# A two-block model of mixers and 16384 experts on one core: how the experts' choice, its weights and the first convolution tap are shared out among the engines

## The chip, the core and the metric

The kernel runs on one core of one Trainium2 chip. The time is the device time of one execution in microseconds, and the median of three runs is compared. The engines are TensorE (PE in the rows), VectorE (DVE), ScalarE (ACT), GpSimd (POOL) and SyncE (SP), which issues most of the transfers.

## What is computed

Two layers of a first block and two of a second, on 256 tokens of width 1024, all in float32. The change touches the first block alone, whose two layers each do:

```python
h = rms_norm(x, norm1_g[l]) * (1.0 + sc1) + sh1
z, xbc, dt_raw, mq, mk, mv, sq, sk, sv = jnp.split(h @ w_in[l], offsets, axis=-1)
# ssd_mixer begins with: xbc = silu(causal_depthwise_conv(xbc, conv_w, conv_b)), 4 taps, 1024 channels
y = concatenate([ssd_mixer(...), moba_attention(...), swa_attention(...)], -1) @ w_out[l]
x = x + g1 * y
h = rms_norm(x, norm2_g[l]) * (1.0 + sc2) + sh2
x = x + g2 * peer_ffn(h, peer_wq[l], peer_k1[l], peer_k2[l], peer_u[l], peer_v[l])
```

and `peer_ffn`, for each token, with 8 heads and 16 of 128 x 128 experts:

```python
q = (xc @ wq).reshape(PEER_CHUNK, PEER_HEADS, 2, PEER_HALF)
s1 = einsum("thd,nd->thn", q[:, :, 0], k1);  s2 = einsum("thd,nd->thn", q[:, :, 1], k2)
v1, i1 = lax.top_k(s1, 16);  v2, i2 = lax.top_k(s2, 16)
cand = (v1[..., :, None] + v2[..., None, :]).reshape(..., 256)
sc, ci = lax.top_k(cand, 16)
e = take(i1, ci // 16) * 128 + take(i2, ci % 16)
g = softmax(sc)
pre = einsum("td,thkd->thk", xc, u[e])
act = gelu(pre) * g
return einsum("thk,thkd->td", act, v[e])
```

## The kernel before

**Parts.** Every weight matrix comes as parts of 128 x 2048 values (1 MB) that SyncE loads into four raw buffers, in one order for the whole kernel. So that TensorE can multiply float32 values in its fast format, each part is split: ScalarE copies it into a rounded upper half (`upper_part`, L1487), and raw minus upper makes the lower half (`lower_part`, L1980 on VectorE, or L766 on GpSimd). There are two buffers for upper halves and two for lower ones, so a lower half of part n can be written only when TensorE is done with part n - 2. TensorE multiplies upper by both halves of the activations and lower by the upper half: `by_feature` (L838, L844) with 32 + 16 matmuls of 256 columns, or `doubled_by_feature` (L886 to L896) with 16 of 512 columns, that take both halves of the activations at once and put them side by side into a bank, and 16 of 256. The second form uses two PSUM banks a part, whose halves must be added afterwards.

**Experts.** All experts are computed densely. 64 parts hold `u` and 64 hold `v`; `expert_order` gives 40 parts of `u` (2 x AHEAD) and then alternates pairs of the two. The gates, a 128 x 128 array for each token that is zero but for the chosen experts, are made as a product of two one-hot matrices (`hot(i)` on VectorE, L2370 and L2371, for eight tokens; `gate_group(i)` on TensorE, L1188; `gates(i)` on ScalarE, L1675), 32 groups a layer. SyncE spills them and fetches them back (`spill`, `fetch`).

**The choice.** While TensorE works on the first LEAD = 21 parts of `u`, VectorE chooses: `best_16` takes maxima, indices and replaced values by groups (L2300 to L2310), first in the 32 groups of scores, then in 16 groups of candidate sums (L2319); then the gate subtraction (L2326), index arithmetic (L2332 to L2343), and two passes of compare, multiply and reduce over 4096 elements (L2347, L2350, L2353) that look up the keys, and the softmax sum, which signals `chosen` (L2359). During this time VectorE makes no lower halves: GpSimd makes those of parts 0 to 22. Then TensorE transposes the chosen numbers (L1178), VectorE copies them (L1960), makes hot(0) and hot(1), and from then on a step is one part and two groups, for 16 steps, and VectorE makes the lower halves again, two parts ahead.

**Ahead of the choice.** The eight query parts (`wq`) are multiplied by `parts_by_feature`, and the results are taken from PSUM by VectorE and ScalarE in turn. When all eight are out, TensorE multiplies by the keys (L1146), eight banks of four groups, and the two engines take these in turn as well. All eight must be out before the first maximum.

**The convolution.** ScalarE takes the four parts of `xbc` into `xpad` (L1578). VectorE then makes four taps in turn (L2109 for the first with the bias, L2112 for the others), with lower halves and the step sizes of the state space part between them; their result is needed for the segment sums (L2156 to L2158 on VectorE, L1046 to L1048 on TensorE).

Order on each engine is that of the program; engines meet only at semaphores. `free`, `filled` and `emptied` are those of a PSUM bank, `p_.upper()`, `p_.lower()`, `p_.lower_free()` and `p_.done()` those of a part.

## Time and profile before

| | us |
|---|---|
| median of three runs | 3445.7 |
| lowest and highest run | 3445.4 and 3454.18 |
| span of the profiled execution | 3444.9 |
| TensorE busy | 3323.0 |
| VectorE busy | 2474.5 |
| ScalarE busy | 1557.9 |
| GpSimd busy | 241.5 |

The busy times are of one profiled execution on the one core, whose mean granted TensorE clock is 0.984 of full speed. A row of a timeline gives the start, the duration, the engine, the line of the kernel, the operation with its output and inputs, how often it stands there, and in brackets the engine's idle time before it and what ended it. Matmuls overlap, so the mean duration of one is longer than the distance to the next.

### The profile page before, as it was taken

The numbers are of one execution on the slowest core, as the hardware profiler recorded it, in microseconds if no ns is written. First come the engines' busy times: TensorE is split into PE (matmuls) and PEld (weight loads), VectorE is DVE, ScalarE is ACT, GpSimd is POOL, SyncE is SP. The second block draws the span as 40 slices with busy tenths as digits, with TensorE's granted clock in tenths as the row PEclk, the third lists the DMA queues.
The fourth block names the chain that finished last, engine by engine and source line by source line (L and its number), as shares of the span: only waits on it lengthen the run. The fifth ranks groups of instructions, "written<-read, shape, count | busy, mean of one in ns | idle before, by whom it ended". The sixth has DMA issues, their size and how long they took to land. (4 is left out here: it accounts for less than half of the span.)

```text
span 3444.9 us, 50906 instructions
## 1 busy us (share of the span) xinstructions
PE 3323.0 (96%) x20214; PEld 2943.0 (85%) x20214; DVE 2474.5 (72%) x4259; ACT 1557.9 (45%) x1835; POOL 241.5 (7%) x56
## 2 busy tenths in 40 slices
PE   7999999999999999999999999999999999999998
PEld 4889999888888899998888878888878788888787
DVE  7879996777887669986667777566657575655575
ACT  3544454343334444454443345453455454544543
POOL 0018400000000039000000000000000000000000
PEclk9999999999999999999999999999999999999999
DMA  9454467778874244566667765543445455434453
GB/s 377 169 181 172 175 224 270 276 275 280 288 272 160 102 167 167 193 238 228 214 213 240 243 251 188 195 147 123 159 150 194 166 205 198 150 133 147 149 188 142
DMA packets 172164, 689.64 MB, mean 200 GB/s; under 512 B 12396, under 2 KB 78724, under 8 KB 99223
## 3 DMA queue, kind: packets, MB, share of 16 engines
q1 hardware_dynamic: 167492, 663.86, 54.4%
q10 hardware_dynamic: 4436, 22.53, 1.8%
q8 instruction: 161, 2.64, 0.3%
q14 instruction: 75, 0.61, 0.0%
HBM read 650.66 MB, written 35.68 MB: 199 GB/s over the span
## 5 line engine op out<-in xcount | busy, mean ns | idle before, releaser
L1487 ACT ACTIVATE weights_upper<-weights 128x2048 fp32r<-128x2048 f32 x520 | 996.1, 1916 | 1546.3 <-issue 467.6
L1980 DVE TENSOR_TENSOR weights_lower<-weights,weights_upper 128x2048 fp32r<-128x2048 f32 x474 | 1084.4, 2289 | 553.2 <-ACT weights_upper L1487 553.0
L838 PE MATMUL ps<-hT_span,weights_upper 128*128 128x256 f32 x4992 | 636.4, 285 | 1.5 <-ACT hT_span L1777 1.2
L838 PEld LDWEIGHTS ps<-hT_span,weights_upper 128*128 128x128 f32 x4992 | 615.1, 193 | 9.0 <-issue 3.5
L890 PE MATMUL ps<-hT_span,weights_upper 128*128 128x512 f32 x1440 | 343.5, 391 | 0.0
L844 PE MATMUL ps<-hT_span,weights_lower 128*128 128x256 f32 x2496 | 325.4, 283 | 4.2 <-POOL weights_lower L766 4.2
L766 POOL TENSOR_TENSOR weights_lower<-weights,weights_upper 128x2048 fp32r<-128x2048 f32 x46 | 238.5, 5200 | 1141.3 <-ACT weights_upper L1487 1141.3
L844 PEld LDWEIGHTS ps<-hT_span,weights_lower 128*128 128x128 f32 x2496 | 310.7, 192 | 5.2 <-POOL weights_lower L766 5.2
L890 PEld LDWEIGHTS ps<-hT_span,weights_upper 128*128 128x128 f32 x1440 | 264.6, 188 | 51.2
L1228 PE MATMUL ps<-weights_upper,hidden_lower 128*128 128x512 f32 x1008 | 250.7, 391 | 0.0
L1228 PE MATMUL ps<-weights_upper,hidden_upper 128*128 128x512 f32 x1008 | 249.0, 389 | 0.0
L1228 PE MATMUL ps<-weights_lower,hidden_upper 128*128 128x512 f32 x1008 | 248.9, 389 | 0.0
L1228 PEld LDWEIGHTS ps<-weights_upper,hidden_lower 128*128 128x128 f32 x1008 | 187.1, 188 | 45.4 <-ACT weights_upper L1487 7.8
L1228 PEld LDWEIGHTS ps<-weights_upper,hidden_upper 128*128 128x128 f32 x1008 | 189.2, 188 | 39.3
L1228 PEld LDWEIGHTS ps<-weights_lower,hidden_upper 128*128 128x128 f32 x1008 | 189.2, 188 | 39.3
L896 PEld LDWEIGHTS ps<-hT_span,weights_lower 128*128 128x128 f32 x1536 | 196.5, 191 | 7.0
L896 PE MATMUL ps<-hT_span,weights_lower 128*128 128x256 f32 x1536 | 199.3, 283 | 0.0
L2371 DVE TENSOR_SCALAR scr<-cst,scr 128x128 f32<-128x128 f32 x512 | 172.2, 336 | 0.0
L2370 DVE TENSOR_SCALAR scr<-cst,scr 128x128 f32<-128x128 f32 x512 | 149.6, 292 | 0.2
L1188 PE MATMUL ps<-scr 128*128 128x128 f32 x1024 | 130.7, 284 | 7.1 <-DVE scr L2371 7.1
L1188 PEld LDWEIGHTS ps<-scr 128*128 128x128 f32 x1024 | 124.4, 198 | 11.1 <-DVE scr L2371 7.8
L2390 DVE TENSOR_TENSOR hidden_upper<-work,scr 128x512 fp32r<-128x512 f32 x80 | 55.4, 692 | 92.8 <-PE ps L1228 92.7
(400 smaller groups left out, 3967.4 us busy)
## 6 DMA issues: line engine op xcount, KB each, us to landing
weights<-in_parts SPq DMA_DIRECT2D x264, 1024.0 KB, 4.8
weights<-in_experts SPq DMA_DIRECT2D x256, 1024.0 KB, 4.9
scr<-gates SPq DMA_DIRECT2D x32, 1024.0 KB, 8.4
work<-in_ada_s SPq DMA_DIRECT2D x96, 256.0 KB, 5.3
gates<-h SPq DMA_DIRECT2D x16, 1024.0 KB, 4.8
gates<-work SPq DMA_DIRECT2D x16, 1024.0 KB, 4.8
weights<-in_ada_w SPq DMA_DIRECT2D x6, 2048.0 KB, 15.3
scr<-in_ada_l SPq DMA_DIRECT2D x35, 256.0 KB, 5.6
```

The lines of the kernel that those rows point to most:

```text
L766: g.tensor_tensor(lower[:, p_.r % SPLIT, :], raw[:, p_.r, :], upper[:, p_.r % SPLIT, :].bitcast(F32), ALU.subtract).then_inc(lower_ready, 1)
L838: m = mm(bank[:, e * T:(e + 1) * T], up[:, c, e * P:(e + 1) * P], s_[:, c, :], start=(e == 0 and n == 0 and c == 0), stop=False, skip_grou ...
L844: m = mm(bank[:, e * T:(e + 1) * T], lo[:, c, e * P:(e + 1) * P], src[0][:, c, :], start=False, stop=(c == KC - 1), skip_group_check=True)
L890: m = mm(banks[e].rearrange("p (n t) -> p n t", n=2), w[:, c, :], both[c], start=(c == 0), stop=False, skip_group_check=True)
L896: m = mm(banks[e][:, T:2 * T], lo[:, c, e * P:(e + 1) * P], src[0][:, c, :], start=False, stop=(c == KC - 1), skip_group_check=True)
L1188: m = mm(k.bank("G", j)[:, t * P:(t + 1) * P], hotA[:, i % 2, 4 * j + t, :], hotB[:, i % 2, 4 * j + t, :], start=True, stop=True, skip_gro ...
L1228: m = mm(k.bank("acc", 2 * t_ + dh), src[:, u, c, t_ * P:(t_ + 1) * P], w[:, c, dh * NBLK:(dh + 1) * NBLK], start=False, stop=False, skip_ ...
L1487: f(upper[:, p_.r % SPLIT, :], raw[:, p_.r, :], ACT.Copy).then_inc(upper_ready, 1)
L1980: v.tensor_tensor(lower[:, s, :], raw[:, p_.r, :], upper[:, s, :].bitcast(F32), ALU.subtract)\
L2370: v.tensor_scalar(hotA[:, i % 2, j, :], iota, ET[:, 0, t:t + 1], None, ALU.is_equal)
L2371: m = v.tensor_scalar(hotB[:, i % 2, j, :], iota, ET[:, 1, t:t + 1], ET[:, 2, t:t + 1], ALU.is_equal, ALU.mult)
L2390: v.tensor_tensor(tokens(hid_up[:, u, :, :]), act_, g_, ALU.mult)
```

## The change

- LEAD is 20 instead of 21, and of the parts before the steady step GpSimd makes only the lower halves 0 to 10 (POOLED = 11). VectorE makes part 11 behind the bit operations, 12 and 13 behind compare and multiply of the first pass, 14 and 15 behind its reduction, 16, 17 and 18 likewise in the second pass, 19 and 20 behind `chosen`, and 21 behind hot(0).
- The gate groups are shifted: group 0 with part LEAD, groups 1 and 2 with the next, and so on (`groups_behind`), and `hot` signals after four tokens instead of eight.
- The query parts use `doubled_by_feature`: 16 fills of a bank instead of 8, ScalarE copies the first half, VectorE adds the second.
- The score banks are filled in the order of the query pieces, each when its four pieces are ready; ScalarE takes all of them, and VectorE takes the first eight maxima of a bank as soon as it is out.
- ScalarE makes the convolution's first tap, two channels' groups behind each take, and the parameters' semaphore is split for it.

```diff
-LEAD = 2 * CHOOSE + 1
+LEAD = 2 * CHOOSE
+POOLED = 11
...
-    p.fill("wq", 8, parts=1)
+    p.fill("wq", 16, last=[i // 2 for i in range(16)])
...
+def groups_behind(n):
+    return range(max(2 * (n - LEAD) - 1, 0), max(min(2 * (n - LEAD) + 1, GROUPS), 0))
...
-                    if 0 <= n - LEAD - RAW < GROUPS // 2:
-                        spill(n - LEAD - RAW)
+                    if 0 <= n - LEAD - RAW - 1 < GROUPS // 2:
+                        spill(n - LEAD - RAW - 1)
                     if n == LEAD + RAW + GROUPS // 2 + 1:
                         fetch(0)
                         fetch(1)
...
                 g.wait_ge(*part(firsts[l], 0, "wq", 7).lower())
-                for n in range(LEAD + SPLIT):
+                for n in range(POOLED):
...
                 for i in range(8):
-                    parts_by_feature(k, 0, "wq", i, src=hT1, fresh=(k, "h2T", "upper1", l * 12 + 8))
+                    doubled_by_feature(k, 0, "wq", i, (k, "h2T", "upper1", l * 12 + 8), src=hT1, both=hT1_both)
                 for i in range(8):
-                    pe.wait_ge(*k.emptied("wq", i))
-                for i in range(8):
-                    t, hp = i // 4, i % 4
+                    hp, t = i // 2, i % 2
+                    for c in range(4 * hp, 4 * hp + 4 if t == 0 else 4 * hp):
+                        pe.wait_ge(*k.emptied("wq", c))
...
-                    pe.wait_ge(S("hot"), l * GROUPS + (i + 1))
                     for j in range(2):
+                        pe.wait_ge(S("hot"), l * (2 * GROUPS) + (2 * i + j + 1))
...
                 for n in range(LEAD, 2 * AHEAD):
                     first_layer(n, *order[n][1:])
-                    if n < LEAD + GROUPS // 2:
-                        for i in range(2):
-                            gate_group(2 * (n - LEAD) + i)
+                    for i in groups_behind(n):
+                        gate_group(i)
...
                     take(k, "xbc", i, xpad[:, 2 * i:2 * i + 2, 3:259])
+                    if i == 0:
+                        act.wait_ge(S("col1_in"), l * 16 + 16)
+                    act.drain()
+                    for c in (2 * i, 2 * i + 1):
+                        m = f(conv[:, c, :], xpad[:, c, 0:T], ACT.Identity, scale=colp[:, K1["cw"] + 4 * c:][:, 0:1],
+                              bias=colp[:, K1["cb"] + c:][:, 0:1])
+                    m.then_inc(S("first_tap"), 1)
...
-                for i in range(1, 8, 2):
-                    ahead("wq", i - 1, 2)
-                    take(k, "wq", i, qT[:, 2 * i:2 * i + 2, :])
+                for i in range(8):
+                    ahead("wq", i)
+                    for e in range(2):
+                        act.wait_ge(*k.filled("wq", 2 * i + e))
+                        act.sem_inc(S("held"), 1)
+                        m = f(qT[:, 2 * i + e, :], k.bank("wq", 2 * i + e)[:, 0:T], ACT.Copy)
+                    m.then_inc(S("wq_first"), 1)
...
-                for i in range(1, 8, 2):
-                    take(k, "s", i, sc[:, 4 * i:4 * i + 4, :])
+                for i in range(8):
+                    g_ = 16 * (i % 2) + 4 * (i // 2)
+                    take(k, "s", i, sc[:, g_:g_ + 4, :])
...
-                for i in range(4):
-                    v.wait_ge(*k.emptied("xbc", i))
-                for tap in range(4):
-                    if tap:
+                for tap in range(1, 4):
+                    if tap > 1:
                         v.drain()
                     for c in range(8):
                         w = colp[:, K1["cw"] + 4 * c + tap:][:, 0:1]
-                        if tap == 0:
-                            m = v.tensor_scalar(conv[:, c, :], xpad[:, c, 0:T], w,
-                                                colp[:, K1["cb"] + c:K1["cb"] + c + 1], ALU.mult, ALU.add)
...
+                        if tap == 1 and c % 2 == 0:
+                            v.wait_ge(S("first_tap"), l * 4 + (c // 2 + 1))
+                        m = v.scalar_tensor_tensor(out=conv[:, c, :], in0=xpad[:, c, tap:tap + T], scalar=w,
+                                                   in1=conv[:, c, :], op0=ALU.mult, op1=ALU.add)
-                    if tap == 0:
+                    if tap == 1:
                         ahead("wint", 0)
-                    elif tap == 1:
                         ahead("wint", 1)
...
-                for i in range(0, 8, 2):
-                    ahead("wq", i, 2)
-                    take(k, "wq", i, qT[:, 2 * i:2 * i + 2, :])
-                    late_pieces(36 + 2 * i, 4 if i < 6 else 0)
-                for i in range(0, 8, 2):
-                    take(k, "s", i, sc[:, 4 * i:4 * i + 4, :])
-
                 for i in range(8):
-                    v.wait_ge(*k.emptied("s", i))
-                v.sem_inc(S("held"), 1)
+                    ahead("wq", i)
+                    late_pieces(36 + 2 * i, 2 if i < 6 else 0)
+                    v.wait_ge(S("wq_first"), l * 8 + (i + 1))
+                    v.sem_inc(S("held"), 1)
+                    for e in range(2):
+                        v.tensor_tensor(qT[:, 2 * i + e, :], k.bank("wq", 2 * i + e)[:, T:2 * T], qT[:, 2 * i + e, :],
+                                        ALU.add).then_inc(k.empty_sem("wq", 2 * i + e), 1)
...
+                for i in range(8):
+                    v.wait_ge(*k.emptied("s", i))
+                    v.sem_inc(S("held"), 1)
+                    g_ = 16 * (i % 2) + 4 * (i // 2)
+                    largest_8(range(g_, g_ + 4), sc, V16)
                 best_16(32, sc, sc2, V16, I16u)
...
+                v.wait_ge(*expert_part(l, 0, POOLED - 1).lower())
+                lower_part(expert_part(l, 0, POOLED))
...
                 for e in range(2):
+                    n = POOLED + 1 + 4 * e
                     v.drain()
                     v.tensor_tensor(onehot[:, :, :], column(Cf[:, e, :], PK), row(iota[:, 0:PK], 256), ALU.is_equal)
+                    lower_part(expert_part(l, 0, n))
...
+                    lower_part(expert_part(l, 0, n + 1))
                     v.drain()
                     v.tensor_reduce(E3[:, e, :], onehot[:, :, :], AX.X, ALU.add)
+                    for i in range(n + 2, n + 4 - e):
+                        lower_part(expert_part(l, 0, i))
...
                 v.tensor_tensor(gate, gate, column(stat(248, 16), PK), ALU.mult).then_inc(S("chosen"), 1)
+                for n in range(POOLED + 8, LEAD + 1):
+                    lower_part(expert_part(l, 0, n))
...
-                    m.then_inc(S("hot"), 1)
+                        if j % 4 == 3:
+                            m.then_inc(S("hot"), 1)
...
                 hot(0)
-                hot(1)
-                v.wait_ge(*expert_part(l, 0, LEAD + SPLIT - 1).lower())
+                lower_part(expert_part(l, 0, LEAD + 1))
...
-                    i = 2 * (n - LEAD) + 2
-                    if i < GROUPS:
+                    for i in groups_behind(n + 1) if n < EXPERTS - 1 else ():
                         hot(i)
-                        hot(i + 1)
```

## Rows read from the trace of the kernel before

**Rows 1.** Page, busy us of an engine (share) xcount; costliest groups: busy, mean ns | idle.

```profile
PE 3323.0 (96%) x20214; PEld 2943.0 (85%) x20214; DVE 2474.5 (72%) x4259; ACT 1557.9 (45%) x1835; POOL 241.5 (7%) x56
...
L1980 DVE TENSOR_TENSOR weights_lower<-weights,weights_upper 128x2048 fp32r<-128x2048 f32 x474 | 1084.4, 2289 | 553.2 <-ACT weights_upper L1487 553.0
```

**Rows 2.** TensorE's waits in the whole span: us in total, times, longest.

```profile
PE ps L1188 <- DVE scr L2371: 7.1, 3, 3.1
...
PE ps L1046 <- DVE scr L2158: 5.9, 2, 4.0
...
PE ps L844 <- POOL weights_lower L766: 4.2, 4, 1.5
...
PE ps L1146 <- ACT work L1470: 1.8, 2, 0.9
```

**Rows 3.** Timeline of TensorE, layer 0: start us, us, engine, line, operation.

```profile
256.40 4.00 PE L838 MATMUL ps<-hT_span,weights_upper 128*128 128x256 f32 x32
...
262.16 4.00 PE L838 MATMUL ps<-hT_span,weights_upper 128*128 128x256 f32 x32
...
374.18 0.82 PE L1178 MATMUL ps<-cst,scr 128*128 128x128 f32 x6
374.76 4.07 PE L838 MATMUL ps<-hT_span,weights_upper 128*128 128x256 f32 x32
...
390.23 4.08 PE L838 MATMUL ps<-hT_span,weights_upper 128*128 128x256 f32 x32
```

**Rows 4.** Windows, one steady step: length, busy us (x) of each engine, clock, DMA.

```profile
390.23:399.74 9.51, 9.51 (x83) 9.40 (x82) 9.51 (x35) 4.81 (x7) 0.00 (x0) 1.00 0.63 221
```

**Rows 5.** Timeline of TensorE, layer 1.

```profile
1260.68 4.00 PE L838 MATMUL ps<-hT_span,weights_upper 128*128 128x256 f32 x32
...
1378.79 0.82 PE L1178 MATMUL ps<-cst,scr 128*128 128x128 f32 x6
...
1395.51 4.49 PE L838 MATMUL ps<-hT_span,weights_upper 128*128 128x256 f32 x32
```

**Rows 6.** Timeline of GpSimd: part 10 of layer 0, last eight parts of layer 1.

```profile
302.80 4.62 POOL L766 TENSOR_TENSOR weights_lower<-weights,weights_upper 128x2048 fp32r<-128x2048 f32 x1 [1.13 <-ACT weights_upper L1487]
...
1335.89 49.01 POOL L766 TENSOR_TENSOR weights_lower<-weights,weights_upper 128x2048 fp32r<-128x2048 f32 x8 [1.01 <-ACT weights_upper L1487]
```

**Rows 7.** Timeline of VectorE, layer 0, second half of the choice.

```profile
309.37 4.10 DVE L2326 TENSOR_TENSOR scr<-scr 128x256 f32<-128x256 f32 x1
...
326.60 8.70 DVE L2347 TENSOR_TENSOR position_hot<-scr,cst 128x4096 bf16<-128x4096 f32 x1
...
342.00 4.42 DVE L2353 TENSOR_REDUCE scr<-position_hot 128x256 f32<-128x4096 bf16 x1
...
375.94 4.43 DVE L2370 TENSOR_SCALAR scr<-cst,scr 128x128 f32<-128x128 f32 x1
```

**Rows 8.** Timeline of VectorE, layer 1: compare and multiply of the first pass.

```profile
1335.50 4.42 DVE L2347 TENSOR_TENSOR position_hot<-scr,cst 128x4096 bf16<-128x4096 f32 x1
1340.00 6.57 DVE L2350 TENSOR_TENSOR position_hot<-position_hot,chosen_keys 128x4096 bf16<-128x4096 bf16 x1
```

**Rows 9.** Timeline of TensorE, second block: two upper passes of the doubled form.

```profile
2061.18 3.82 PE L890 MATMUL ps<-hT_span,weights_upper 128*128 128x512 f32 x16
...
2066.75 3.82 PE L890 MATMUL ps<-hT_span,weights_upper 128*128 128x512 f32 x16
```

**Rows 10.** Groups of instructions by line: busy us, mean ns | idle before.

```profile
L1470 ACT ACT_TABLE_LOAD x8 | 10.3, 1283 | 0.1
...
L1660 ACT ACTIVATE work<-ps 128x256 f32<-128x256 f32 x24 | 7.8, 376 | 0.0
```

**Rows 11.** Timeline of ScalarE, layer 1, behind the xbc parts.

```profile
1096.44 1.92 ACT L1487 ACTIVATE weights_upper<-weights 128x2048 fp32r<-128x2048 f32 x1 [2.34 <-PE ps L941]
```

**Rows 12.** Timeline of VectorE, layer 1: the first tap and the second weight part.

```profile
1091.58 2.67 DVE L2109 TENSOR_SCALAR work<-work,colp 128x256 f32<-128x256 f32 x8
...
1099.72 2.29 DVE L1980 TENSOR_TENSOR weights_lower<-weights,weights_upper 128x2048 fp32r<-128x2048 f32 x1
```

24 lines of the change are left out of this document (12 added, 12 removed).

## The prediction, made before the changed kernel ran

> **What bounds the kernel.** I read the page's table of busy time first: TensorE is busy for 96% of the span [rows 1], so the time is the matrix work plus the places where TensorE waits. The view of waits then names them, and the ones this change can touch are four [rows 2]: L1188 (gate groups) on VectorE's one-hots, 7.1 us; L844 (lower parts) on GpSimd, 4.2 us; L1146 (key scores) on ScalarE, 1.8 us; L1046 (segment sums) on VectorE, 5.9 us, 4.0 of it in layer 1, so 1.9 in layer 0. Waits understate a stall, since steps between them stretch too; so I took TensorE's timeline around the choice and compared it with its own rhythm. A first-layer part takes 5.76 us from start to start [rows 3]. Part 1 begins at 256.40, so part 21 would come 20 x 5.76 = 115.2 us later, at 371.6; the transposes L1178 that precede it start at 374.18: 2.6 us lost. From there to part 22 at 390.23 are 16.05 us. The same work undisturbed is 0.58 (transposes, 374.18 to 374.76) and one full step with two gate groups, 9.51 [rows 4]: 10.09. So 6.0 more are lost, 8.6 in layer 0. Layer 1 [rows 5]: 1378.79 against 1260.68 + 115.2 = 1375.9 is 2.9; 16.72 against 10.09 is 6.6; 9.5 together. In the steady step VectorE is busy for all its 9.51 us, so TensorE and VectorE are level there [rows 4], and nothing is to be had in it.
>
> **Why it is lost.** GpSimd's subtraction takes 4.62 us when alone, on TensorE's beat of 5.76. But the last eight, in layer 1 from 1335.89, take 49.01 us, 6.1 each [rows 6]. VectorE's side shows the partner [rows 7]: the gate subtraction at 309.37 ends at 313.47, just behind GpSimd's part 11 (302.80 + 5.76 + 4.62 = 313.18); the compare of 4096 elements takes 8.70 at 326.60, and 4.42 in layer 1 where GpSimd asks only afterwards [rows 6, 8]; the multiply takes 6.57 [rows 8]; the first one-hot at 375.94 takes 4.43, where the 32 of a steady step have (9.51 - 2.29) / 32 = 0.23 each [rows 1, 4], and it holds up hot(0) and so the gate groups. Each long row is its own work plus the rest of a GpSimd instruction. The Trainium skill (SBUF, State Buffer, "two separate sides") has this as a rule: the port pair that VectorE and GpSimd share is locked for a whole instruction, and an operation with two SBUF inputs takes part in it. The rows agree.
>
> **The change, part by part**
>
> 1. **Lower parts 11 to 21 on VectorE.** GpSimd keeps 0 to 10. Part 10 at 302.80 ends at 307.42 [rows 6], before the gate subtraction. From there no VectorE operation meets GpSimd. I cost the late choice in that state: from the gate subtraction to the compare 17.23 us now, of which the gate's own wait is 313.18 - 309.37 = 3.8 and two more GpSimd instructions of 4.62 are waited for (parts 12 and 13, the cast L2334 and L2339), so 4.2 remain; then for each of two passes compare 4.42, multiply, reduce 4.42 [rows 7, 8]. The multiply is bounded by 6.57 above; in layer 1 the compare ends at 1339.92, GpSimd then works 4.62 to 1344.5, and the multiply that began at 1340.00 ends at 1346.57 [rows 8], which leaves 2.0. I take 2.1. (The Trainium skill, VectorE: DVE Perf Modes, in its tier table, gives two-input bf16 work twice the fp32 rate, an estimated 2.1 for 4096 elements; same term.) Added are subtractions of 2.29 each [rows 1].
>    In TensorE's layer 0 times: part n's lower half can be made from 308.56 + 5.76 (n - 11) (GpSimd's own starts), when the buffer and upper half are there, and must be made by the middle of part n, 256.40 + 5.76 (n - 1) + 3.84. Gate at 309.4, part 11 done 312.8 (needed 317.8); compare ends about 320.4, part 12 at 322.6 (323.6); multiply, 13 at 327.0 (329.4); reduce, 14 at 333.7 (335.1), 15 at 336.0; compare, 16 at 342.8 (346.6); multiply, 17 at 347.2 (352.4); reduce, 18 at 353.9 (358.2). "chosen" comes near 355, 19 at 357.3, 20 waits for its buffer until 360.4 and ends 362.7. TensorE reaches the transposes at 256.40 + 19 x 5.76 = 365.8. Everything fits, parts 12 and 14 by 1.0 and 1.4 us only.
> 2. **One part earlier, groups shifted.** VectorE copies the transposes and starts hot(0) 1.8 behind their start (375.94 against 374.18 [rows 3, 7]), so hot(0) runs 367.6 to 371.3: a group costs (9.51 - 2.29) / 2 = 3.6 [rows 1, 4]. TensorE is in part 20 until 372.2 and finds group 0 ready. Then 21 lower, hot(1), hot(2) end near 383.0; TensorE wants the second half of group 2 at 382.7. About 0.3 is lost, and only because the signal now comes per four tokens; per eight it would be 1.3. All the 8.6 and 9.5 go except that: 8.3 + 9.2 = **17.5 us**. The reordered spill and fetch keep their place relative to the groups; a fetch one step earlier stands in SP's queue ahead of a raw load that is needed three parts later, so nothing.
> 3. **Wide query pieces.** Seven of eight parts change to the form of L886/L890, whose step is 2066.75 - 2061.18 = 5.57 [rows 9] against 5.76: 0.19 x 7 = 1.3 a layer, **2.7 us**. ScalarE now makes two copies of 256 per part at 0.38 [rows 10] and VectorE two adds beside the 2.29 and two late pieces, under 5.57; hidden.
> 4. **Scores in order of pieces.** The first scores no longer need the last query, so L1146's waits go, **1.8 us** [rows 2]. ScalarE takes all eight score banks behind two upper parts of 1.92 [rows 11]; the first eights of the maxima run bank by bank beside them instead of in one piece behind the last. The choice is about 3 us earlier against TensorE. I credit nothing: the next cast and additions need the shared pair, which GpSimd holds 4.62 of every 5.76 us, and the early start lands inside such a hold that ends where the work begins now.
> 5. **First tap on ScalarE.** VectorE loses 2.67 us of L2109 [rows 12]. In layer 1 the second weight part behind it is tied to ScalarE's upper part at 1096.44 + 1.92 [rows 11], so its start moves from 1099.72 [rows 12] to 1098.5: **1.2 us**. In layer 0 the whole 1.9 us of L1046's wait can go: **1.9 us**. ScalarE's eight 256-wide operations, about 0.38 each [rows 10], lie in its waits. No Identity stands in this trace: a table load for it is bounded by 0 and the 1.28 that the others take [rows 10]; I take 0. The Trainium skill (ScalarE: Activation LUTs, "Table sets") puts identity into every set, so by it too the term is 0.
>
> **Sum:** 17.5 + 2.7 + 1.8 + 3.1 = 25.1 us. The profiled execution's span is 3444.9, the median of the runs 3445.7, so 0.8 lies around the span; the removal applies to both. 3445.7 - 25.1 = 3420.6; I say **3421**. TensorE is the bound behind every place touched, so the gain is handed on.
>
> **The rivals**
>
> - **A lock met in the first half** (chance 0.27). The two candidate additions are back to back. If the shifted chain lets GpSimd in between, they end 4.6 later, the whole late choice too, and part 12, with 1.0 of room, is 3.6 late in each layer in which it happens. 3.6 to 7.2 back: 3424 to 3428. For: GpSimd's beat is fixed to TensorE and the choice moves by 3 us against it. Against: the chain starts from the same end of hold as before. If the multiply costs 4.4 instead of 2.1, it comes to a similar 1 to 2 a layer. By the skill's rule as worded, whoever asks first gets the pair for a whole instruction; that makes this rival a matter of tenths of a microsecond in the asking, worth the same 3.6 a layer.
> - **The small edits bring nothing** (0.12): table loads around each Identity (8 x 1.28 a layer on ScalarE, up to 6.0 in a 5.76 step), or the mixer's earlier start is waited away later. 3.1 to 5 back: 3424 to 3426.
> - **Slower: the long durations belong to the operations** (0.04). If 8.7, 6.5, 4.1, 5.1, 4.9 us stay without GpSimd, the gate to part 12 grows by 4 + 4.6 + 4.6 + 4.3 = 17.5 against 1.0 of room, and each later pass by some 4.3 + 4.5; part 20 would be some 27 us late instead of 8.6 to 9.5. That is 18 a layer more than now, 36 in all, less the 7.6 of the other edits: about 3474. It decides from the moment when the extra exceeds part 12's room plus the 8.6 won. Against it speaks the 4.42 in layer 1 [rows 8], and that each long row ends with GpSimd's.
> - **No change to be measured** (0.05): VectorE becomes the bound between gate and chosen through unseen costs (drains, waits for upper parts, since VectorE now stands still in order behind a lower part), 8 to 9 us a layer, all that part 2 wins less the rest: about 3438 to 3444.
>
> **How the numbers follow.** The forecast has 0.52, with its own range 3417 to 3424 (multiply, 0 to 0.5 us of waits in the ramp, tap gain 0 to full, a little more if the granted clock, 0.98 overall, gains from fewer pauses). The range for 8 in 10 takes in the first two rivals and part of the last: 3416 to 3433. A measurement tells 0.3%, 10.3 us, from no change. Faster by more than that: 0.52 + 0.27 + 0.12 = 0.91; within: 0.05; slower: 0.04.
>
> **What would show it.** GpSimd has 22 instructions, nearly all at 4.6 us; the compare 4.4, multiply 2.1, gate and first one-hot 0.3. The waits of L844 on GpSimd are gone and no wait of L844 or ScalarE on VectorE's lower parts takes their place; if one does, at part 12 or 14, the first rival holds. L1188's waits shrink from 7.1 to under 1. Query parts step by 5.57, L1146 waits for nothing, L1046 waits 2.8 in layer 1 and 0 in layer 0, no table load stands beside Identity. The forecast is wrong if compare or multiply keep their length, or if TensorE is held inside parts 11 to 20.

## The result: 3418.0 us, 28 less than before, and the profile after

The changed kernel takes 3418.01 us (median of four runs, 3416.88 to 3418.65), the kernel before 3445.98 on the same chip: a ratio of 0.9913, 95% interval 0.9901 to 0.9926. The forecast was 3421 with 25.1 us won; 28.0 were. The median lies in the range of 3416 to 3433, but the ratio, applied to the 3445.7 of the table above, gives 3415.7, just under its lower end. It is the ratio of the means, and those of the kernel before hold the one run of 3454.18; the ratio of the medians is 0.9919 and gives 3417.7. Run again later (e9), the changed kernel had 3418.89 us against 3447.24, a ratio of 0.9916. So the forecast was some 3 us short both times, and that has to be accounted for.

Page of the changed kernel, busy us (share) and two groups of instructions, against [rows 1]:

```profile
PE 3312.6 (97%) x19990; PEld 2923.9 (86%) x19990; DVE 2452.1 (72%) x4283; ACT 1575.4 (46%) x1883; POOL 106.1 (3%) x32
...
L1998 DVE TENSOR_TENSOR weights_lower<-weights,weights_upper 128x2048 fp32r<-128x2048 f32 x498 | 1139.0, 2289 | 553.7 <-ACT weights_upper L1494 553.4
...
L773 POOL TENSOR_TENSOR weights_lower<-weights,weights_upper 128x2048 fp32r<-128x2048 f32 x22 | 103.1, 4691 | 1186.8 <-ACT weights_upper L1494 1186.8
```

TensorE's waits in the whole span, against [rows 2] (TensorE's lines of the kernel have moved on by 7 or 8, VectorE's by up to 29):

```profile
PE ps L1053 <- DVE scr L2172: 2.7, 1, 2.7
...
PE ps L1196 <- DVE scr L2400: 0.4, 2, 0.2
```

Lower halves and key scores are waited for no more, the gate groups wait 0.4 us instead of 7.1, and the segment sums wait once, in layer 1.

TensorE's timeline, layer 0 (start, duration, line, operation, [wait]), against [rows 3]:

```profile
203.69 3.82 PE L897 MATMUL ps<-hT_span,weights_upper 128*128 128x512 f32 x16
...
209.25 3.82 PE L897 MATMUL ps<-hT_span,weights_upper 128*128 128x512 f32 x16
...
245.55 4.40 PE L845 MATMUL ps<-hT_span,weights_upper 128*128 128x256 f32 x32
...
361.15 0.82 PE L1186 MATMUL ps<-cst,scr 128*128 128x128 f32 x6
361.72 4.07 PE L845 MATMUL ps<-hT_span,weights_upper 128*128 128x256 f32 x32
365.63 2.08 PE L851 MATMUL ps<-hT_span,weights_lower 128*128 128x256 f32 x16
367.55 1.95 PE L1196 MATMUL ps<-scr 128*128 128x128 f32 x16
369.25 4.08 PE L845 MATMUL ps<-hT_span,weights_upper 128*128 128x256 f32 x32
...
378.31 1.16 PE L1196 MATMUL ps<-scr 128*128 128x128 f32 x8 [0.20 <-DVE scr L2400]
```

Query parts step by 5.56 us. From part 0 (245.55) to the transposes (361.15) TensorE stands nowhere; behind them the whole ramp (the first gate groups, until the steady step is reached) costs one wait of 0.20, the 0.3 of the forecast.

VectorE, layer 0: the candidates, then the late choice, against [rows 7]:

```profile
280.38 0.43 DVE L2333 CAST chosen_keys<-scr 128x512 bf16<-128x512 uint32 x1
280.72 6.31 DVE L2338 TENSOR_TENSOR work<-scr 128x768 f32<-128x768 f32 x2
...
304.17 0.43 DVE L2346 TENSOR_TENSOR scr<-scr 128x256 f32<-128x256 f32 x1
...
311.04 4.43 DVE L2370 TENSOR_TENSOR position_hot<-scr,cst 128x4096 bf16<-128x4096 f32 x1
315.38 2.29 DVE L1998 TENSOR_TENSOR weights_lower<-weights,weights_upper 128x2048 fp32r<-128x2048 f32 x1
317.76 2.29 DVE L2374 TENSOR_TENSOR position_hot<-position_hot,chosen_keys 128x4096 bf16<-128x4096 bf16 x1
```

Gate 0.43 for 4.10, compare 4.43 for 8.70, multiply 2.29 for 6.57. But the two additions took 6.31, against 1.88 in layer 1: they met GpSimd, which is the first rival's event. A meeting, here and below, is a VectorE operation that is long by the rest of a GpSimd subtraction. GpSimd's row at the same place:

```profile
280.83 5.32 POOL L773 TENSOR_TENSOR weights_lower<-weights,weights_upper 128x2048 fp32r<-128x2048 f32 x1 [1.14 <-ACT weights_upper L1494]
```

It is 0.7 us longer than the usual 4.62: GpSimd waited out the first addition (0.95 us from 280.72), and the second then waited out GpSimd (5.45 us from 281.59). In layer 1 the cast waits instead:

```profile
1274.35 3.63 DVE L2333 CAST chosen_keys<-scr 128x512 bf16<-128x512 uint32 x1
1277.91 1.88 DVE L2338 TENSOR_TENSOR work<-scr 128x768 f32<-128x768 f32 x2
```

**Where the 28 us are.** I cut the TensorE timeline at landmarks that every version has: its first xbc part; the first segment sum; part 0 of the experts (U0); the zeroing of the accumulators behind the u parts and the ramp; layer 1's first transposes; the first scaled transposes of the second block; TensorE's end. Two stretches are left out of the table because they are the same in every trace: from the zeroing of layer 0 to layer 1's first transposes 511.5 us, from that of layer 1 to the second block 492.7. The lengths, in us, of all kernels (the labels are explained below):

| kernel | start | xbc to seg | seg to U0 | U0 to zero | L1: to seg | seg to U0 | U0 to zero | 2nd block |
|---|---|---|---|---|---|---|---|---|
| before | 54.67 | 52.41 | 143.17 | 299.92 | 51.56 | 141.59 | 300.95 | 1387.43 |
| before, e8 | 55.04 | 53.19 | 144.75 | 300.24 | 51.55 | 141.68 | 301.14 | 1387.31 |
| e4 | 54.36 | 52.53 | 143.15 | 298.85 | 51.56 | 142.35 | 298.91 | 1387.33 |
| e10 | 55.34 | 52.34 | 143.17 | 298.91 | 51.55 | 142.29 | 299.87 | 1381.37 |
| after | 54.15 | 50.72 | 140.68 | 291.75 | 50.25 | 139.04 | 291.43 | 1385.60 |
| after, e9 | 54.42 | 50.11 | 140.60 | 291.56 | 50.23 | 139.08 | 291.25 | 1386.59 |
| e7 | 54.57 | 50.20 | 140.57 | 291.59 | 50.22 | 139.10 | 291.28 | 1377.59 |
| e1 | 54.24 | 52.48 | 143.11 | 291.63 | 51.58 | 142.32 | 296.90 | 1385.92 |
| e5 | 54.15 | 52.58 | 143.15 | 291.58 | 51.57 | 141.50 | 295.39 | 1387.31 |
| e14 | 54.85 | 52.50 | 144.77 | 296.97 | 51.58 | 142.63 | 296.84 | 1386.26 |
| e2 | 54.27 | 50.10 | 140.57 | 298.94 | 50.25 | 138.95 | 298.72 | 1384.45 |
| e3 | 55.10 | 50.12 | 140.60 | 298.08 | 50.25 | 137.66 | 297.62 | 1386.62 |
| e6 | 54.73 | 50.12 | 143.00 | 291.60 | 50.22 | 139.87 | 291.30 | 1387.89 |
| e11 | 54.89 | 50.35 | 140.71 | 293.41 | 50.22 | 139.18 | 293.10 | 1386.73 |
| e12 | 53.90 | 50.11 | 140.58 | 292.51 | 50.24 | 137.44 | 292.17 | 1385.19 |
| e13 | 53.79 | 50.96 | 140.68 | 293.35 | 50.25 | 140.32 | 293.56 | 1384.52 |
| e15 | 53.88 | 50.14 | 140.57 | 297.48 | 50.26 | 139.00 | 296.83 | 1380.69 |

Between the first "before" and the first "after" row: choice 8.2 and 9.5 (forecast 8.3 and 9.2), tap 1.7 and 1.3 (1.9 and 1.2), query and score edits 2.5 and 2.55 (2.25 each), start 0.5 and second block 1.8, neither of them touched by the change. The last two make 2.3 of the missing 3 us. 1.6 of the second block is one place, its boundary. The rows of L779 or L786 are fillers: multiplications without use that TensorE does while it waits. Before, then after:

```profile
2041.91 3.68 PE L779 MATMUL ps<-cst 128*128 128x512 f32 x8
2048.46 5.41 PE L810 MATMUL ps<-diag,x_res 128*128 128x128 f32 x32 [2.87 <-DVE diag L2499]
```

```profile
2015.66 3.68 PE L786 MATMUL ps<-cst 128*128 128x512 f32 x8
2022.21 3.81 PE L817 MATMUL ps<-diag,x_res 128*128 128x128 f32 x32 [2.87 <-DVE diag L2526]
```

Same work, same pause of 2.87 us ahead of it, 5.41 against 3.81 us. So two theories went into the experiments: the 3 us are the granted clock behind pauses; and, since the additions did meet GpSimd and nothing was lost by it, the 3 us earlier start of the choice, which I had credited with nothing, is what paid for the meeting.

### The profile page after: what moved, and what is told of

Read it like the earlier page. It is cut to its first block and busy times, and to the rows that moved or that the text cites. A ratio compares the mean times of both kernels' runs of the same rounds, so it can differ in the third digit from the quotient of the medians.

```text
span 3416.8 us, 50647 instructions
## 1 busy us (share of the span) xinstructions
PE 3312.6 (97%) x19990; PEld 2923.9 (86%) x19990; DVE 2452.1 (72%) x4283; ACT 1575.4 (46%) x1883; POOL 106.1 (3%) x32
## 5 line engine op out<-in xcount | busy, mean ns | idle before, releaser
L1998 DVE TENSOR_TENSOR weights_lower<-weights,weights_upper 128x2048 fp32r<-128x2048 f32 x498 | 1139.0, 2289 | 553.7 <-ACT weights_upper L1494 553.4
L845 PE MATMUL ps<-hT_span,weights_upper 128*128 128x256 f32 x4480 | 570.9, 285 | 1.6 <-ACT hT_span L1795 1.3
L845 PEld LDWEIGHTS ps<-hT_span,weights_upper 128*128 128x128 f32 x4480 | 550.7, 192 | 9.5 <-issue 3.9
L897 PE MATMUL ps<-hT_span,weights_upper 128*128 128x512 f32 x1664 | 396.9, 391 | 0.0
L897 PEld LDWEIGHTS ps<-hT_span,weights_upper 128*128 128x128 f32 x1664 | 305.8, 188 | 59.2
L851 PE MATMUL ps<-hT_span,weights_lower 128*128 128x256 f32 x2240 | 291.6, 283 | 0.0
L1235 PEld LDWEIGHTS ps<-weights_upper,hidden_upper 128*128 128x128 f32 x1008 | 189.2, 188 | 39.3
L1235 PEld LDWEIGHTS ps<-weights_lower,hidden_upper 128*128 128x128 f32 x1008 | 189.2, 188 | 39.3
L773 POOL TENSOR_TENSOR weights_lower<-weights,weights_upper 128x2048 fp32r<-128x2048 f32 x22 | 103.1, 4691 | 1186.8 <-ACT weights_upper L1494 1186.8
```

Of the source, the lines that this page charges most:

```text
L773: g.tensor_tensor(lower[:, p_.r % SPLIT, :], raw[:, p_.r, :], upper[:, p_.r % SPLIT, :].bitcast(F32), ALU.subtract).then_inc(lower_ready, 1)
L845: m = mm(bank[:, e * T:(e + 1) * T], up[:, c, e * P:(e + 1) * P], s_[:, c, :], start=(e == 0 and n == 0 and c == 0), stop=False, skip_grou ...
L851: m = mm(bank[:, e * T:(e + 1) * T], lo[:, c, e * P:(e + 1) * P], src[0][:, c, :], start=False, stop=(c == KC - 1), skip_group_check=True)
L897: m = mm(banks[e].rearrange("p (n t) -> p n t", n=2), w[:, c, :], both[c], start=(c == 0), stop=False, skip_group_check=True)
L1235: m = mm(k.bank("acc", 2 * t_ + dh), src[:, u, c, t_ * P:(t_ + 1) * P], w[:, c, dh * NBLK:(dh + 1) * NBLK], start=False, stop=False, skip_ ...
L1998: v.tensor_tensor(lower[:, s, :], raw[:, p_.r, :], upper[:, s, :].bitcast(F32), ALU.subtract)\
```

## The experiments

Each version ran beside the kernel before, whose medians were then 3445.2 to 3447.9 us; ratios are against those.

**e1, the choice stage alone** (the change without first tap, wide query pieces, score order and maxima by bank):

```
-LEAD = 2 * CHOOSE + 1
+LEAD = 2 * CHOOSE
+POOLED = 11
...
+                v.wait_ge(*expert_part(l, 0, POOLED - 1).lower())
+                lower_part(expert_part(l, 0, POOLED))
```

> The kernel before with the choice stage of the change alone: GpSimd makes lower parts 0 to 10 and VectorE the rest, the choice is used one part earlier, the gate groups are shifted and signalled per four tokens. The whole change moved TensorE's choice stages by 8.2 us in layer 0 and 9.5 us in layer 1. Theory (the terms of the prediction add up, and the 3 us that it had not forecast are another cause): 17.7 us less than before, 3427.5 to 3429 against 3445.9. Rival (the choice stage is worth more than counted, since its pauses also lower TensorE's granted clock elsewhere): 20 us or more less, 3426 or below. Rival (the small edits are needed for it, because the choice starts later without them): gate about 3 us later against TensorE, waits on VectorE inside parts 12 to 14, 12 to 15 us less, above 3430.

Measured: 3434.15 us, 12.8 less; ratio 0.9964 (0.9950 to 0.9977). Neither 17.7 nor more: the third case, in one layer only. Layer 0 wins 8.3 as in the changed kernel, layer 1 only 4.05. VectorE and TensorE, layer 1:

```profile
1286.52 0.43 DVE L2319 CAST chosen_keys<-scr 128x512 bf16<-128x512 uint32 x1
1286.86 6.32 DVE L2324 TENSOR_TENSOR work<-scr 128x768 f32<-128x768 f32 x2
```

```profile
1323.88 3.12 PE L851 MATMUL ps<-hT_span,weights_lower 128*128 128x256 f32 x16 [3.80 <-DVE weights_lower L1985]
```

The gate comes 63.4 us behind U0 instead of 59, and TensorE waits 3.80 us for lower part 12. The first rival is real, and its price here is 5.6 us (296.90 against 291.3), not 3.6: behind the wait the lower pass takes 3.12 us for 2.08 and the next upper pass 4.59 for 4.00, at a granted clock of 0.72 from 1323.8 to 1330.

**e2, the small edits alone** (e1's complement: tap, wide query pieces, scores, maxima).

> The kernel before with the other edits alone: wide query pieces, scores in order of pieces with the maxima bank by bank, and the first tap on ScalarE; the choice stage as before. By TensorE's times in the changed kernel they moved layer 0 by 1.7 + 2.5 and layer 1 by 1.3 + 2.5 us. Theory: 8.0 us less than before, 3437 to 3439, and the two choice stages lose the same 8.6 and 9.5 us as before. Rival (VectorE's chain through the choice, 3 us earlier here, gives some of it back, or the shift is eaten): 4 to 6 us less, 3440 to 3442.

Measured: 3431.84 us, 15.1 less; ratio 0.9961 (0.9948 to 0.9975). The theory's 8.0 is half of it. By the table their own places give 2.3 + 2.6 + 1.3 + 2.6, 8.9 us unrounded, for the 8.0 expected. The rest of the span's 15.4 lies where they do nothing: 1.0 and 2.2 in the choice stages, where the transposes come hardly earlier against U0 (by 0.01 and 0.35) and the ramp behind them is shorter, 3.0 in the second block, 0.4 at the start. Both of the ranges expected were missed. That e1 and e2 add up to 27.9, as the whole does, is chance; and against e2 the choice stage is worth 13.0 us in the medians (3431.84 against 3418.89) and 14.9 in the table, less than the 17.7 of the first pair of traces.

**e3, GpSimd makes all lower parts** of the choice stage in the changed kernel:

```
-                for n in range(POOLED):
+                for n in range(LEAD + 2):
...
-                lower_part(expert_part(l, 0, POOLED))
```

> The changed kernel with GpSimd making all 22 lower parts of the choice stage (0 to 21), VectorE none; one part earlier, shifted groups, per four tokens and all small edits stay. Theory (the loss is the shared hold of VectorE and GpSimd, so the split of the lower parts is what wins): the gate, compare and multiply operations again take 4 to 9 us, the choice ends 10 us or more late in each layer, and most of the 17.7 us come back: 3432 to 3440, since the choice is also needed 5.8 us earlier than in the kernel before. Rival (the shift of the groups wins most of it): under 6 us come back, below 3424.

Measured: 3431.73 us; ratio 0.9955 (0.9941 to 0.9968): 12.8 us come back against e9. The theory holds: the long rows are the meeting, not the operation. VectorE's compare and TensorE's transposes, layer 0:

```profile
322.17 8.70 DVE L2368 TENSOR_TENSOR position_hot<-scr,cst 128x4096 bf16<-128x4096 f32 x1
```

```profile
366.77 1.41 PE L1186 MATMUL ps<-cst,scr 128*128 128x128 f32 x6 [2.64 <-DVE scr L2380]
```

**e4, fillers into the pause at the block boundary** of the kernel before:

```
-                    scaled_transposes(k, f + "T", (l * 4 + n) * TT, busy=2 if n else 4)
+                    scaled_transposes(k, f + "T", (l * 4 + n) * TT, busy=2 if n else 6)
```

> The kernel before with four more filler multiplications of TensorE (two steps of the filler, 0.46 us each) ahead of the scaled transposes that begin the first feed-forward of each layer of the second block, so that they fill 1.8 us of the 2.87 us in which TensorE waits there. Nothing else changes, and VectorE's result comes when it came before. Theory (the 1.57 us that the changed kernel won at this place beyond the forecast are TensorE's granted clock, 0.5 there before and 1.0 after): the 32 multiplications take 3.8 instead of 5.4 us, and the kernel is 1.5 us faster, 3444.4 against 3445.9, or a little more. Rival (the 5.4 us are due to something beside them, such as the DMA load): they still take 5.4 us and the time is unchanged.

TensorE at the boundary:

```profile
2039.36 5.40 PE L779 MATMUL ps<-cst 128*128 128x512 f32 x12
2045.91 3.81 PE L810 MATMUL ps<-diag,x_res 128*128 128x128 f32 x32 [1.16 <-DVE diag L2499]
```

3.81 instead of 5.41 us. Windows of the two stretches, the kernel before, then e4 (columns as in [rows 4]):

```profile
2048.00:2053.00 5.00, 4.54 (x26) 4.57 (x27) 0.74 (x3) 1.48 (x4) 0.00 (x0) 0.66 1.00 421
2045.00:2050.00 5.00, 4.05 (x34) 3.87 (x34) 1.41 (x7) 3.07 (x9) 0.00 (x0) 1.00 1.00 419
```

The DMA engines are as full in both, so they are not the reason; the granted clock is, 0.66 against 1.00. That the fillers brought it, one trace can't show: of the thirteen traces without them six have the fast form too (after, e9, e1, e14, e3, e12: 3.6 us to the next instruction) and seven the slow one (5.0 to 5.2). All four with them (e4, e10, e7, e15) are fast. The median of 3444.37 (ratio 0.9996, 0.9987 to 1.0005) can't be told from no change.

e4 shows one thing more. Its first block is that of the kernel before, yet its two choice stages take 298.85 and 298.91 us, not 299.92 and 300.95. Windows 133.5 to 140 us behind U0 of layer 1, the kernel before, then e4:

```profile
1388.35:1394.85 6.50, 5.53 (x29) 5.24 (x30) 6.50 (x22) 1.79 (x3) 0.00 (x0) 0.60 0.00 0
1387.84:1394.34 6.50, 4.83 (x40) 4.64 (x41) 6.50 (x22) 2.40 (x4) 0.00 (x0) 1.00 0.00 0
```

Both stand behind the same wait of 3.1 us for VectorE. So up to 3.1 us of the loss that was read from the first trace was low clock in the ramp, which another execution doesn't have.

**e8, the kernel before again**, for a second trace.

> The kernel before once more, unchanged, for a second profiled execution. Theory (where the granted clock falls is not fixed by the program: the same wait is followed by a stretch at 0.5 in one execution and not in another): the waits are the same to 0.1 us, but the stretches of low clock stand at partly other places, and TensorE's milestones shift by 1 to 2 us between the two executions around the gate groups and the boundary of the second block. Rival (they are fixed by the program): all milestones agree within 0.3 us.

The span is 3448.1 against 3444.9 (3450.2 us in its one run). 2.7 of the 3.2 us arise before U0 of layer 0. The waits of the gate groups are the same 7.1 us, but TensorE waits 2.93 us instead of 1.95 for the first segment sum. At the segment sums of layer 0, windows of 104 to 114 us, first this execution, then the first one (columns as in [rows 4]):

```profile
104.00:114.00 10.00, 7.07 (x44) 6.67 (x43) 9.61 (x24) 9.44 (x14) 0.00 (x0) 0.83 0.43 159
```

```profile
104.00:114.00 10.00, 8.05 (x66) 7.75 (x65) 9.51 (x23) 9.27 (x12) 0.00 (x0) 1.00 0.55 209
```

Clock 0.83 against 1.00 in the same program: stretches at 1.2 instead of 2.4 GHz are not at fixed places. But the wait ahead of this one was 1.0 us longer too, so it doesn't show one and the same wait with two clocks behind it; the thirteen boundaries above do show that, over several kernels. My guess of the places was wrong (gate groups and boundary agree within 0.4 us here). Single runs of the kernel before say the same as the two traces: beside e14, one took 3443.39 us at a mean granted clock of 0.987 and one 3449.37 at 0.984.

**e7, fillers into every pause** of the changed kernel ahead of hT (layer 1), h2T, nT and the four feed-forward transposes:

```
-                    transposes(k, "hT", h, "h1", l * TT, busy=5)
+                    transposes(k, "hT", h, "h1", l * TT, busy=7 if l else 5)
...
-                transposes(k, "h2T", h, "h2", l * TT, busy=2)
+                transposes(k, "h2T", h, "h2", l * TT, busy=5)
...
-                    scaled_transposes(k, f + "T", (l * 4 + n) * TT, busy=2 if n else 4)
+                    scaled_transposes(k, f + "T", (l * 4 + n) * TT, busy=5 if n or l else 6)
...
-                scaled_transposes(k, "nT", (l * 4 + 1) * TT, busy=3)
+                scaled_transposes(k, "nT", (l * 4 + 1) * TT, busy=5)
```

> The changed kernel with more filler multiplications of TensorE (0.46 us each, two a step) ahead of the transposes for which it waits for VectorE: 2 steps more ahead of layer 1's first transposes, 3 ahead of h2T in both layers, 2 ahead of the first feed-forward (1 in layer 1), 3 ahead of the second, 2 ahead of nT; each lies inside a wait of 1.8 to 3.9 us that is there anyway. Theory (behind such a wait TensorE often runs at a granted clock of 0.5, in the changed kernel behind five of them, and each such stretch costs about 1.5 us): the transposes behind the filled waits run at full clock, 5 to 8 us less than the changed kernel's 3418.0, so 3410 to 3413. Rival (the clock falls elsewhere instead, or the fillers themselves are paid for): 3416.5 to 3420.

Measured: 3410.32 us; ratio 0.9900 (0.9885 to 0.9915), the fastest version, 7.7 less than the changed kernel. TensorE ahead of nT, the changed kernel, then e7:

```profile
2210.12 2.74 PE L786 MATMUL ps<-cst 128*128 128x512 f32 x6
2215.55 4.66 PE L817 MATMUL ps<-diag,x_res 128*128 128x128 f32 x25 [2.70 <-DVE diag L2526]
2219.82 1.17 PE L817 MATMUL ps<-diag,x_res 128*128 128x128 f32 x9
```

```profile
2209.59 4.45 PE L786 MATMUL ps<-cst 128*128 128x512 f32 x10
2215.03 3.81 PE L817 MATMUL ps<-diag,x_res 128*128 128x128 f32 x32 [0.98 <-DVE diag L2526]
```

5.23 us (2215.55 to 2220.78) become 3.58 (2215.03 to 2218.61). Here the fillers are the cause: this place takes 5.0 to 6.5 us in all fourteen traces without them, and 3.6 in all three with them (e7, e10, e15). The gain is in the second block (1377.59 against 1385.60 and 1386.59); up to its first transposes e7 is 0.5 us ahead of one trace of the changed kernel and 0.3 behind the other.

**e10, the same fillers in the kernel before.**

> The kernel before with the same added fillers of TensorE as the filled version of the changed kernel (3410.3 us): fewer stretches of low clock behind waits, the choice stage as before. Theory (the change without these accidents is worth the terms of the sum with their measured sizes, 25.1 forecast plus 0.5 for the query and score edits): 25.6 us above 3410.3, so 3435 to 3437, and 9 to 10 us under the kernel before. Rival (the change is worth 28 us whatever the clock does elsewhere): 3438 to 3439.

Measured: 3442.07 us (3435.38 to 3445.65, 11 runs); ratio 0.9987 (0.9978 to 0.9996): both numbers missed, the distance to e7 is 31.8 us. By the traces the first block agrees with the theory: up to the second block's first transposes e10 is 25.95 us behind e7 (2047.65 against 2021.70), after against before 26.25. The other 3.8 lie in the second block (1381.37 against 1377.59), where both kernels are the same, and the profiled run (3440.1) was faster than the median. That part I can't assign. The same fillers are worth 5.2 us here (against 3447.24), 7.7 in the changed kernel.

**e9, the changed kernel again.**

> The changed kernel once more, unchanged, for a second profiled execution and more times. Theory (of the 3 us beyond the forecast, 1.57 at the boundary of the second block and 0.5 at the start are accidents of the granted clock in the one execution of the kernel before that was read, and 0.5 are the query and score edits): the time scatters from 3416 to 3420 with a median near 3418.5, and from the first scaled transposes of the second block to the second ones TensorE takes either 193.3 or some 194.9 us. Rival (the boundary always keeps its clock in the changed kernel): 193.3 us again and a median of 3418.0 or below.

Measured: 3418.89 us (3417.28 to 3419.77); ratio 0.9916 (0.9903 to 0.9930), as the theory has it; the boundary took 193.3 us again (2021.44 to 2214.76), so it can't tell the theories apart there. e11 does: its boundary took 194.9.

**e6, the changed kernel without the query, score and maxima edits.**

> The changed kernel without the wide query pieces, the order of the scores and the maxima by bank (three edits undone together); choice stage and first tap as in the changed kernel. Theory A (these edits are worth their own 2.5 us a layer, and besides they start the choice 3 us earlier, which is room that a meeting with GpSimd needs): 5 us lost plus 3.8 us in each layer in which the additions meet GpSimd, so 3423 with no meeting, 3427 with one, 3431 with two; the gate comes 59 us behind part 0 without a meeting and 63.4 with one. Theory B (as in the prediction, the earlier start is worth nothing): 5 us lost in all, 3423, whatever the additions meet.

Measured: 3423.40 us; ratio 0.9933 (0.9919 to 0.9947). No meeting took place (gate at 59.1 and 58.8), so the two theories, which give 3423 both for that, stay untold apart. The edits are worth 4.5 us against e9, 3.2 of them in their own places by the table and 1.3 in the second block. Its choice stages are as long as e9's (291.60 and 291.30 against 291.56 and 291.25): the earlier start, which it lacks, is worth nothing as long as no meeting comes. Against e1, from which it differs by the tap alone, it is 10.7 us faster: in e1 the cast of layer 1 stood 39.6 us behind U0, here 39.3, and that 0.3 us decided on the meeting. The tap isn't the reason for it, since the kernel before has 39.3 as well; in e1 and e5 the first maxima start 0.37 us later, behind ScalarE's last score copy, and why that is late stays open.

**e5, e1 with lower part 12 ahead of the first compare** (and no longer behind it):

```
+                lower_part(expert_part(l, 0, POOLED + 1))
                 for e in range(2):
...
+                    if e:
+                        lower_part(expert_part(l, 0, n))
```

> The kernel with the choice stage of the change alone (the one that took 3434.15 us), with one more edit: VectorE makes lower part 12 ahead of the first compare instead of behind it. In layer 1 of that kernel the two candidate additions met GpSimd (6.32 us instead of 1.88), the gate came 63.4 us behind TensorE's part 0 instead of 58.6, and TensorE then waited 3.80 us for lower part 12. Theory (what the choice alone lacks against the 17.7 us is this one late part, since without the query and score edits the choice begins 3 us later against TensorE and has no room for a meeting with GpSimd): part 12 is done 2.2 + 2.2 us earlier, the wait of 3.80 goes, 4 to 5 us less in layer 1, 3429 to 3430.5. Rival (the whole chain is late, and the lateness is only handed to part 13 or to part 20 and the one-hots): 0 to 1 us less, 3433 to 3434.5.

Measured: 3433.85 us; ratio 0.9965 (0.9951 to 0.9979). My theory fell: the lateness goes to the next part, for which TensorE waits 2.59 us at 1327.61. The chain is late as a whole, and an order behind the gate doesn't mend it.

**e14, e1 with the additions ahead of the cast:**

```
-                v.tensor_copy(keys[:, :, :, :], I16u.rearrange("p (g e) k -> p g e k", e=2))
                 ...
                                     ALU.add)
+                v.tensor_copy(keys[:, :, :, :], I16u.rearrange("p (g e) k -> p g e k", e=2))
                 v.drain()
```

> The choice stage of the change alone (3434.15 us) with the cast of the chosen keys moved behind the two candidate additions. In layer 1 of that kernel the cast ran at 39.6 us behind part 0 and took 0.43, the additions began at 40.0 and met GpSimd, 6.32 instead of 1.88 us. Theory (who asks for the pair first gets it: the additions now ask 0.4 us earlier, ahead of GpSimd's hold that begins at 40.0): the additions take 1.88 us and GpSimd begins late instead, the gate comes 59 us behind part 0, the wait of 3.80 us for lower part 12 goes: 4 to 5 us less, 3429 to 3430. Rival (the additions meet GpSimd's hold anyway, or the lateness has another source): 3433 to 3434.5, additions 4 to 6 us.

Measured: 3440.78 us; ratio 0.9983 (0.9974 to 0.9992), 6.6 slower than e1. VectorE, layer 1, and TensorE in both layers:

```profile
1294.46 1.90 DVE L2323 TENSOR_TENSOR work<-scr 128x768 f32<-128x768 f32 x2
1296.28 4.85 DVE L2327 CAST chosen_keys<-scr 128x512 bf16<-128x512 uint32 x1
```

```profile
329.22 3.55 PE L851 MATMUL ps<-hT_span,weights_lower 128*128 128x256 f32 x16 [3.60 <-DVE weights_lower L1985]
...
1331.81 2.83 PE L851 MATMUL ps<-hT_span,weights_lower 128*128 128x256 f32 x16 [3.78 <-DVE weights_lower L1985]
```

In layer 1 the additions ran free, as expected, but GpSimd got in behind them and the cast met it; in layer 0 both waited, the additions with 3.77 us and the cast with 4.84. The gate is at 63.6 and 63.4 either way, and each layer loses 5.4 and 5.5 us (296.97 and 296.84 against 291.6 and 291.3). So a meeting with this subtraction of GpSimd's, the one that begins 41 us behind U0, is the cause, and which operation suffers it doesn't matter.

**e13, the gate made late** (changed kernel, 2.72 us of searches done twice):

```
                 best_16(16, cand, sc_c, Vc, Cu)
+                largest_8(range(16), cand, Vc)
+                v.drain()
```

> The changed kernel with VectorE made 2.8 us late on purpose: the 16 searches of the largest eight of the candidates (2.72 us) are done a second time right ahead of the gate subtraction. Theory (part 12 is the tight one, with 1.2 us of room in the changed kernel, and all else in the choice stage has more): TensorE waits about 1.6 us for lower part 12 in each layer and for nothing else there, 3.2 us more, 3421.5 to 3423, up to 3425 if the clock falls behind the wait. Rival (the earlier start by the query and score edits is not needed, the chain has more room than I read): under 1 us more, 3419 to 3420.

Measured: 3422.46 us; ratio 0.9933 (0.9919 to 0.9946), 3.6 above e9. The gate is 2.8 and 2.7 later, and in the choice stages TensorE waits for lower part 12 alone:

```profile
320.44 2.17 PE L851 MATMUL ps<-hT_span,weights_lower 128*128 128x256 f32 x16 [1.49 <-DVE weights_lower L1998]
...
1316.12 2.17 PE L851 MATMUL ps<-hT_span,weights_lower 128*128 128x256 f32 x16 [2.04 <-DVE weights_lower L1998]
```

So the room was 2.8 - 1.49 = 1.3 and 2.7 - 2.04 = 0.7 us; the forecast had 1.0.

**e15, e7 with the additions ahead of the cast.**

> The filled version of the changed kernel (3410.3 us) with the same order, additions ahead of the cast. Theory: in layer 0 the additions at 34.8 us behind part 0 no longer meet GpSimd (1.88 instead of 6.32 us), the gate comes up to 4 us earlier unless it then meets GpSimd's last part, and since TensorE waits for nothing in the choice stage the time is the same, 3409.5 to 3411.5. Rival (an earlier gate meets GpSimd's part 10 and is thrown back, or a new meeting makes a part late): above 3413.

Measured: 3421.22 us; ratio 0.9923 (0.9910 to 0.9937), 10.9 slower than e7. Here the additions (6.33 and 5.10) and the cast (4.85 twice) both wait, the gate comes at 63.1 and 63.4, and each layer loses 5.5 to 5.9 us. The rival holds: the 3 us of earlier start pay for one meeting, not for two.

**e11, no shift of the groups** (spills moved along):

```
-LEAD = 2 * CHOOSE
+LEAD = 2 * CHOOSE + 1
...
-    return range(max(2 * (n - LEAD) - 1, 0), max(min(2 * (n - LEAD) + 1, GROUPS), 0))
+    return range(max(2 * (n - LEAD), 0), max(min(2 * (n - LEAD) + 2, GROUPS), 0))
...
                 hot(0)
+                hot(1)
```

> The changed kernel with the choice used where it was used before: the transposes stand ahead of part 21, not 20, and each part has its two gate groups behind it, both made ahead; VectorE still makes lower parts 11 to 22, signals per four tokens. Theory (what wins is that VectorE and GpSimd no longer meet; the shift by a group covers only VectorE's two first groups, 7.2 us from 1.8 us behind the transposes against TensorE's 6.4): 0.3 to 1 us lost in each layer, 3418.5 to 3420.5, no wait of 3.1 us of the gate groups. Rival (the shift is what removes the ramp): waits of 3 us at the first gate groups and low clock behind them as before, 4 us or more a layer, 3426 or above.

Measured: 3423.56 us; ratio 0.9929 (0.9915 to 0.9943), 4.7 above e9; 1.8 us a layer by the table. Five waits of at most 0.7 us, none of 3.1: nearer to the theory, but outside both ranges; the shift is worth nearly twice the 1 us a layer that I allowed.

**e12, one signal per eight** (TensorE waits once for a group):

```
-                        pe.wait_ge(S("hot"), l * (2 * GROUPS) + (2 * i + j + 1))
+                        pe.wait_ge(S("hot"), l * GROUPS + (i + 1))
...
-                        if j % 4 == 3:
-                            m.then_inc(S("hot"), 1)
+                    m.then_inc(S("hot"), 1)
```

> The changed kernel with one signal for eight one-hot pairs instead of four. Theory (working of the prediction: 0.3 us are lost in the ramp with a signal per four, 1.3 with one per eight): TensorE waits 1.0 to 1.3 us at gate group 2 instead of 0.2, 1.0 us more a layer, 3419.5 to 3421. Rival (VectorE hands group 2 over early enough, or a wait of 1 us lowers the clock too): 3418 or 3423 and more.

Measured: 3421.03 us; ratio 0.9925 (0.9912 to 0.9939), 2.1 above e9; one wait of 1.26 us a layer, 0.9 us each by the table. As worked out, at the upper end of the range.

## Why the prediction was right, and where it fell short

1. **Lower parts on VectorE, groups shifted: 17.5 forecast, 17.7 measured** in the first pair of traces. That agreement is in part luck: the loss was read from an execution with low clock in both ramps. Against e4's and e2's traces, with the same choice stage as before, the part is worth 14.5 to 15.0, so up to 3 us of it are clock and not the order of the work. e3 shows the cause (12.8 back without the split), e11 the share of the shift (1.8 a layer), e12 the price of the signal (0.9 for 1.0). The multiply took 2.29 for 2.1. The late choice kept its timetable: part 12 was done at 317.67, 72.1 us behind U0; the prediction has 322.6, 72.4 behind U0 (250.25).
2. **Wide query pieces and scores: 4.5 forecast, 5.0 measured.** Step 5.56 for 5.57, no wait at the scores.
3. **First tap: 3.1 forecast, 3.0 in that pair of traces, 3.6 in the usual lengths** (52.4 to 50.1 and 51.56 to 50.24). Two Identity operations take 1.10 us, 0.55 each for the 0.38 assumed, and no table load was added (one of 1.28 us stands behind them, that of L1550, which the kernel before has as well).
4. **The first rival was misjudged, without effect on the number.** It put a meeting at 3.6 us a layer. One did happen in layer 0 (6.31 us) and cost nothing: the cast begins 34.8 us behind U0 and the additions end at 41.5, while in the kernel before the cast begins at 37.9, waits out the same subtraction of GpSimd's, and the additions end at 42.0. So the credit of nothing was right as far as it went, and for the reason given: the gate comes at 58.6 and 59.0 against 59.1 and 58.8 before, and e6 without the earlier start loses nothing in its choice stages. What the prediction lacked is what the start guards against. A chain that is 0.3 us later than usual is thrown behind GpSimd's next subtraction, and that costs 5.4 to 5.6 us, not 3.6 (e1, and the reordered chain of e14); in e15 the reordered chain is thrown back in spite of the early start. So the small edits guard the large one.
5. **The step that failed: everything outside the five edits was put at nothing, with "a little more" for the granted clock.** So the own range ended at 3417 and the wide one at 3416, 4 to 5 us below the forecast, with the edits' own terms to be covered too. 28.1 us went between the two spans, for 25.1: 0.5 came at the start and 1.8 in the second block, where nothing was changed, and 0.5 in the query and score stage. At the boundary (1.6 of the 1.8) it is the clock, by the windows of e4; elsewhere it is not shown place by place. In the second pair of medians the surplus is there again (28.4), so it is not one odd execution, and both traces of the kernel before are slow at the boundary, both of the changed one fast. In the thirteen traces of kernels with an unchanged second block it took 1384.5 to 1387.9 us, before at the long end both times, which is not enough to say whether the change has a part in it. The low end should have been some 3 us lower for this alone.

Of the losses read as waits in the ramp, a part was clock too. Windows of the kernel before, then after, behind the first gate groups:

```profile
384.00:390.00 6.00, 6.00 (x30) 5.87 (x31) 6.00 (x19) 1.56 (x3) 0.00 (x0) 0.54 0.01 4
```

```profile
378.00:385.00 7.00, 6.80 (x58) 6.69 (x57) 7.00 (x23) 2.80 (x3) 0.00 (x0) 1.00 0.82 300
```

Granted 0.54 behind a wait of 3.10 us. Measuring the loss against TensorE's own rhythm, not by the sum of its waits, took that in without knowing it, and with it the part that is an accident of one execution (e4).

## What to carry to other kernels

A loss is best read as the distance between landmarks against the undisturbed rhythm; that sum held within 0.6 us a term in the first pair of traces, while medians of whole runs moved by 3 us for reasons elsewhere. But one trace of the kernel before is not enough for it: the same choice stages took up to 3.1 us less in another one. A second trace before the forecast would have given the range its width. Where two engines exclude each other, room ahead of the tight operation is worth as much as a shorter operation: look how late the chain may come, and which edit gives it that room (1.3 and 0.7 us here, e13). TensorE's pauses cost twice, once as a wait and once as slow work behind it; filler work inside them won 7.7 us here, as much as the three small parts of the change were forecast to win, and 5.2 in the kernel before.
